# The last expert passes of a hybrid decoder step: the last gate ahead of the second square, one table change, and the scaling of two token tiles given to GpSimd and ScalarE

## The reference

```python
def rmsnorm(x, g):
    y = x * lax.rsqrt(jnp.mean(x * x, axis=-1, keepdims=True) + 1e-6)
    return y * g

# x: (536, 1024) after the mixer; u = rmsnorm(x, norm2_g)
h = (silu(einsum('btd,edf->btef', u, expert_w_gate))      # 16 experts, d = 1024, f = 256
     * einsum('btd,edf->btef', u, expert_w_up))
h = h * combine[..., None]                                # the top 1 of 4 groups, the top 2 in it
x = x + einsum('btef,efd->btd', h, expert_w_down)
y = rmsnorm(x, final_norm_g)
```

## Time and profile before

| | us |
|---|---|
| median of 3 runs | 812.83 (811.8 to 813.1) |
| the profiled execution | 816.96 |
| its span | 815.3 |
| PE busy (matmuls) | 782.8 (96%) |
| DVE busy | 431.7 (53%) |
| ACT busy | 208.4 (26%) |
| POOL busy | 38.8 (5%) |
| DMA moved | 126.89 MB, mean 156 GB/s |

### The profile page before, as it was taken

How to read it: one execution, slowest core, us unless ns; L and a number is a source line. 1 busy time by engine, 2 the same in 40 slices (tenths; PEclk the granted TensorE clock), 3 DMA queues, 4 the chain that set the end, 5 groups by cost and what they waited for, 6 DMA issues and landing times.

```text
span 815.3 us, 19720 instructions
## 1 busy us (share of the span) xinstructions
PE 782.8 (96%) x8426; PEld 539.0 (66%) x8426; DVE 431.7 (53%) x856; ACT 208.4 (26%) x488; POOL 38.8 (5%) x49
## 2 busy tenths in 40 slices
PE   7999999999999999999999999999999789999984
PEld 6877777787767877777777877767788533333321
DVE  5775667588768565657566455356114431111225
ACT  3122222254523312221212332220022401111134
POOL 0000000000000000000000000000000112222121
PEclk9999999999999999999999999999999889999997
DMA  9531432432212101201230102073935689999963
GB/s 341 202 113 51 137 107 71 176 105 65 91 52 80 53 28 55 68 15 61 81 104 28 51 32 80 2 266 162 384 116 207 220 326 400 390 403 393 349 224 136
DMA packets 36389, 126.89 MB, mean 156 GB/s; under 512 B 5736, under 2 KB 16008, under 8 KB 31440
## 3 DMA queue, kind: packets, MB, share of 16 engines
q1 hardware_dynamic: 32416, 115.78, 37.8%
q0 software_dynamic: 3888, 9.87, 4.3%
HBM read 106.31 MB, written 18.68 MB: 153 GB/s over the span
## 4 chain that ended last, share of the span: by engine, by line
PE 89%; DVE 4%; DMA 3%; issue 2%; ACT 1%; SPq 0%; POOL 0%; POOLq 0%; DVEq 0%; ACTq 0%
PE psum L1357 23%; PE psum L1338 12%; PE psum L1677 9%; PE psum L2554 9%; PE psum L2586 4%; PE psum L1315 4%; PE psum L1291 2%; PE psum L1302 2%; PE psum L1545 2%; PE psum L1633 1%; DVE arena L2019 1%; PE psum L1558 1%; PE psum L2534 1%; PE psum L1377 1%; PE psum L1442 1%
## 5 line engine op out<-in xcount | busy, mean ns | idle before, releaser
L2019 DVE TENSOR_TENSOR arena<-arena 128x512 f32<-128x512 f32 (+10 forms) x312 | 170.3, 546 | 50.8 <-ACT arena L1776 31.5
L1357 PE MATMUL psum<-arena 128*128 128x268 f32 x784 | 189.5, 393 | 0.0
L1357 PEld LDWEIGHTS psum<-arena 128*128 128x128 f32 x784 | 145.1, 189 | 37.8 <-issue 11.6
L1776 ACT ACTIVATE arena<-psum 128x268 f32<-128x268 f32 (+4 forms) x213 | 84.9, 406 | 282.6 <-PE psum L1357 146.6
L2019 DVE TENSOR_TENSOR arena<-psum,arena 128x256 f32<-128x256 f32 (+5 forms) x170 | 71.7, 425 | 80.9 <-PE psum L1558 21.8
L1338 PE MATMUL psum<-arena 128*128 128x268 f32 x392 | 105.0, 402 | 0.0
L1677 PE MATMUL psum<-arena 128*128 128x268 f32 x384 | 91.0, 391 | 1.6 <-DVE arena L2019 1.2
L2554 PE MATMUL psum<-arena 128*32 128x512 f32 (+1 forms) x640 | 86.2, 601 | 0.5 <-DVE arena L2707 0.3
L1338 PEld LDWEIGHTS psum<-arena 128*128 128x128 f32 x392 | 69.7, 189 | 20.4 <-issue 6.3
L1677 PEld LDWEIGHTS psum<-arena 128*128 128x128 f32 x384 | 71.1, 189 | 17.7 <-issue 3.3
L2707 DVE TENSOR_TENSOR arena<-psum,arena 128x256 f32<-128x256 f32 (+2 forms) x38 | 24.3, 663 | 104.4 <-ACT arena L2621 90.9
(11 more groups left out here) (205 smaller groups left out, 710.0 us busy)
## 6 DMA issues: line engine op xcount, KB each, us to landing
arena<-in_w_gu SPq DMA_DIRECT2D x16, 2048.0 KB, 21.6
arena<-in_w_in SPq DMA_DIRECT2D x46, 512.0 KB, 4.3
arena<-in_w_dn SPq DMA_DIRECT2D x16, 1024.0 KB, 20.6
arena<-in_w_out SPq DMA_DIRECT2D x2, 2048.0 KB, 14.6
arena<-arena SPq DMA_DIRECT2D x5, 536.0 KB, 5.2
arena<-in_x SPq DMA_DIRECT2D x8, 268.0 KB, 4.6
arena<-arena SPq DMA_DIRECT2D x16, 134.0 KB, 4.3
arena<-in_x SPq DMA_DIRECT2D x1, 2144.0 KB, 14.5
```

The source lines that it names most:

```text
L1357: last = mm(ps, w[:, k, :], x[:, k, :], start=(k == 0 and i in (0, 1, 3)), stop=(k == KD // 2 - 1), skip_group_check=i not in (0, 1, 3))
L1776: run(nc.scalar.activation(out, in_, fn, **kw), s)
L2019: run(v.tensor_tensor(out, a, b, op), s)
```

## The change

Four things change, all in the loop's last part.

1. ScalarE: `gate(11)` and `hidden_out(10)` come behind square(0) and ahead of the one Sqrt table load; root(0) comes after that, then squares and roots 1 and 2, then `hidden_out(11)`.
2. VectorE: `hidden(11)` comes ahead of all norms. `summed(0)`, with its wait for all late gathers, comes ahead of normed(2); summed(1) ahead of normed(4). For tiles 3 and 4 `normed` does only the reciprocal.
3. GpSimd: the three late gathers are issued only when tiles 0 and 1 have landed. When the gathers have landed, GpSimd multiplies tiles 3 and 4 by `g_row` into `ug`. ScalarE scales them by the reciprocal root with a Copy, in place, between its squares (`scaled(t)`), and SyncE writes these two to y from `ug`.
4. Two semaphores are new: `z_gx` (GpSimd to ScalarE) and `z_gy` (ScalarE to SyncE).

```diff
--- before.py
+++ after.py
@@ -49,6 +49,7 @@
 LATER = HT - EARLY * P
 LG0, PS0, ID0 = 0, 192, 320
 LATE = 3
+GAINED = 3
 SHIFT_TILES = 14
 RET0, GA0, GB0 = 14, 30, 38
 
@@ -939,6 +940,8 @@
         z_rt = sem("z_rt")
         z_rc = sem("z_rc")
         z_y = sem("z_y")
+        z_gx = sem("z_gx")
+        z_gy = sem("z_gy")
         z_out = [sem(f"z_out{i}") for i in range(2)]
 
         def rows_of(t):
@@ -2471,10 +2474,15 @@
                         n = rows_of(t)
                         sp.dma_start(xf[0:n, t, :], x2_dram[t * P:t * P + n, :]).then_inc(z_x[t], 16)
                     for t in range(TT):
-                        at_least(sp, z_y, TT + LATE, t + 1)
+                        n = rows_of(t)
+                        if t < GAINED:
+                            at_least(sp, z_y, GAINED + LATE, t + 1)
+                            y = xf[0:n, t, :]
+                        else:
+                            at_least(sp, z_gy, TT - GAINED, t - GAINED + 1)
+                            y = ug[0:n, t - GAINED, :]
                         sp.nop(nofuse=True)
-                        n = rows_of(t)
-                        sp.dma_start(O["y"][t * P:t * P + n, :], xf[0:n, t, :]).then_inc(z_out[t % 2], 16)
+                        sp.dma_start(O["y"][t * P:t * P + n, :], y).then_inc(z_out[t % 2], 16)
                     for j in range(LATE):
                         at_least(sp, z_late[j], 16, 16)
                     sp.nop(nofuse=True)
@@ -2504,19 +2512,25 @@
                                                 compute_op=ALU.add).then_inc(q_yd[e % 2], 16)
                     for q in range(2):
                         then(q_yd[q], ADDS[q], ADDS[q])
+                    then(z_x[0], 16, 16)
+                    then(z_x[1], 16, 16)
                     for j in range(LATE):
                         e = FIRST_LATE + j
                         pool.indirect_dma_start(late[:, j, :], None, x2_dram,
                                                 bass.IndirectOffsetOnAxis(ap=ids[:, e:e + 1], axis=0),
                                                 bounds_check=T - 1, oob_is_err=False).then_inc(z_in, 16)
                     then(z_in, 16 * LATE, 16 * LATE)
-                    for t in range(TT):
+                    then(z_x[2], 16, 16)
+                    then(q_tr, PIECES, parts_in(NPASS - 1))
+                    for t in range(GAINED, TT):
                         then(z_x[t], 16, 16)
+                        n = rows_of(t)
+                        nc.gpsimd.tensor_tensor(ug[0:n, t - GAINED, :], xf[0:n, t, :], g_row[0:n, :], ALU.mult).then_inc(z_gx, 1)
 
                     then(z_out[0], 48, 48)
                     then(z_out[1], 48, 48)
                     for j in range(LATE):
-                        then(z_y, TT + LATE, TT + j + 1)
+                        then(z_y, GAINED + LATE, GAINED + j + 1)
                         e = FIRST_LATE + j
                         pool.indirect_dma_start(O["y"], bass.IndirectOffsetOnAxis(ap=ids[:, e:e + 1], axis=0), fin[j], None,
                                                 bounds_check=T - 1, oob_is_err=False).then_inc(z_late[j], 16)
@@ -2662,30 +2676,29 @@
                         if i:
                             hidden_out(i - 1)
                             rows_out(i - 1)
-                    tables = [0]
-
-                    def table(fn):
-                        if tables[0]:
-                            at_least(act, z_sq, 3, tables[0])
-                        a(dummy, eps2[:, :], fn).then_inc(z_sq, 1)
-                        tables[0] += 1
-
                     gate(NPASS - 2)
                     hidden_out(NPASS - 3)
-                    table(ACT.Sqrt)
-                    for t in range(2):
+                    square(0)
+                    gate(NPASS - 1)
+                    hidden_out(NPASS - 2)
+                    a(dummy, eps2[:, :], ACT.Sqrt).then_inc(z_sq, 1)
+                    root(0)
+                    for t in range(1, 3):
                         square(t)
                         root(t)
-                    table(ACT.Sigmoid)
-                    gate(NPASS - 1)
-                    hidden_out(NPASS - 2)
-                    table(ACT.Sqrt)
-                    square(2)
-                    root(2)
                     hidden_out(NPASS - 1)
+                    def scaled(t):
+                        n = rows_of(t)
+                        at_least(act, z_gx, TT - GAINED, t - GAINED + 1)
+                        at_least(act, z_rc, TT + LATE, t + 1)
+                        y = ug[0:n, t - GAINED, :]
+                        a(y, y, ACT.Copy, scale=rs[0:n, t:t + 1]).then_inc(z_gy, 1)
+
                     for t in range(3, TT + 2):
                         square(t)
                         root(t)
+                        if GAINED < t <= TT:
+                            scaled(t - 1)
                     x = late[:, LATE - 1, :]
                     at_least(act, z_half, 1, 1)
                     at_least(act, z_ss, TT + LATE, squares[0])
@@ -2743,6 +2756,8 @@
                         n = x.shape[0]
                         at_least(dve, z_rt, TT + LATE, norms[0])
                         v.reciprocal(rs[0:n, t:t + 1], rs[0:n, t:t + 1]).then_inc(z_rc, 1)
+                        if GAINED <= t < TT:
+                            return
                         at_least(dve, z_rc, TT + LATE, norms[0])
                         v.scalar_tensor_tensor(y, x, rs[0:n, t:t + 1], g_row[0:n, :], ALU.mult, ALU.mult).then_inc(z_y, 1)
 
@@ -2765,15 +2780,15 @@
                                             AX.X, ALU.add).then_inc(q_ws, 1)
                         if 0 < i < NPASS - 2:
                             rows_in(i + 1)
+                    hidden(NPASS - 1)
                     normed(0)
                     normed(1)
-                    hidden(NPASS - 1)
-                    normed(2)
                     at_least(dve, z_in, 16 * LATE, 16 * LATE)
                     summed(0)
+                    normed(2)
                     normed(3)
+                    summed(1)
                     normed(4)
-                    summed(1)
                     normed(TT)
                     for q in range(2):
                         x = late[:, LATE - 1, 512 * q:512 * q + 512]
```

## The result

The changed kernel takes 818.08 us (median of 6 runs, 817.15 to 819.04), the kernel before 813.15 us beside it; the ratio is 1.0048, 95% interval 1.0032 to 1.0065. It is slower by 0.48%, where 0.25% less was forecast; 818.08 lies outside the range of 809.0 to 814.3. In the profiled executions the spans are 815.4 and 815.3 us, so two things have to be explained: what the change does in its trace, and why the kernel before is usually 3 to 4 us faster (medians of 812.8 to 813.8 us) than the execution of 816.96 us that the prediction was made on.

A forecast was written before the change was run, and what follows sets the result against it. It took TensorE's hole before down(10), then VectorE, then GpSimd's three scatters to bound the end. Down(11) gains 4.7 us, over half lost again; the third scatter starts 2.0 us sooner, 810.8 us for the median, range 809.0 to 814.3.

The forecast's parts named there:

- the first term of the sum: Last gate moved ahead on ScalarE: TensorE's idle 3.11 us before down(10) go, and the clock's fall (1.57 us) with them.
- L: Time when all late gathers are in, which summed(0) and GpSimd's products wait for: 794.3, 3.6 us after the last issue.
- the gathers are late: Rival: late gathers land later, delaying the end one to one; at 799.6 the time is 816.1 us; chance 0.12.
- Products and exclusion: GpSimd's two products take 2.6 us each and exclude VectorE products with two SBUF inputs; normed(2) held from 795.8 to 797.4.
- One table load: On ScalarE three loads of 1.28 us become one; its queue is through some 4 us sooner, which alone moves no end.
- The clock: TensorE's granted clock stays at 1.00 up to 799, without the fall to 0.50 behind the hole before down(10).

The follow-up runs named there:

- a_free_vector: The changed kernel with gathers issued as before and all five token tiles normed on VectorE: 813.75 us, ratio 1.0000 against the kernel before.
- a_store: The changed kernel with the first store of y held until the gathers have landed: 815.59 us, ratio 1.0016 against the kernel before.
- a_free: The changed kernel with its gathers issued as before, ahead of the landing of tiles 0 and 1: 814.28 us, ratio 1.0003 against the kernel before.
- c_early: The changed kernel, gathers issued as before, summed(0) waiting for the first alone, GpSimd products ahead of its wait for the gathers: 812.61 us, ratio 0.9982.
- b_wait: The kernel before with only the two GpSimd waits added (gathers issued once tiles 0 and 1 have landed): 816.63 us, ratio 1.0036.
- a_vector: The changed kernel with all five token tiles normed on VectorE, gathers still late: 817.34 us, ratio 1.0043 against the kernel before.
- a_norm_late: The changed kernel with normed(0) and normed(1) behind summed(0) on VectorE: 820.24 us, ratio 1.0079 against the kernel before.
- b_again3: The kernel before, unchanged, in a fourth profile: one execution of 814.10 us.
- b_again2: The kernel before, unchanged, in a third profile: one execution of 816.31 us.

## Why the prediction was wrong, point by point

- **The baseline.** The sum was made against one execution, of the late form, and I took the difference over to the median as if form and median had nothing to do with each other. That execution was 4.1 us over the median of the runs, and I noted it without asking what it was. In the early form the gate is in time by itself. So moving it, the first term of the sum, is right in its trace (gate at 786.7, no hole, down(10) 3.66 us), and no gain over the median was measured for it: a_free_vector, which has it together with the one table load and the new order, is at 1.0000 (0.9990 to 1.0010). That the median is of the early form is argued, as said above.
- **The step that failed: L.** "From issue to landing ... I take near the low end, 3.6" was 7.3 us. The issues themselves were right (787.05 is g+7.5, forecast g+7.25), and tile 1 alone did come early. Of the 3.7 us between them 0.8 is there in a_store too, where only the gathers move then (4.4 us). Another 0.8 is the third issue, which took 1.77 us beside VectorE's norm of tile 0 (789.38 to 790.66); I had read that very hindrance off the scatter in the earlier trace rows and applied it only to the products. The rest, up to 2.1 us, goes to the stores of y tiles 0 and 1, which the later gathers now meet. The earlier trace rows had them: of q1's 2.10 MB in 787 to 797 only 1.06 MB were tiles by my own count, so the other 1.04 MB were these two stores. I used them for the rate and left them out of what had still to move. With them, 3.18 MB at 0.32 MB/us from 787 on give 797.0 for the last gather in place of 793.7, an estimate that is 1.2 us under what came (g+16.2 against g+17.5). L came 3.9 us later than forecast, counted from g.
- **The rival "the gathers are late"** was the case that happened, with 0.12. Its rule, one to one in L, gives g+31.9 for the last scatter (27.95 + 3.9); 31.2 was measured. With the right L the sum is 0.7 us off, profile against profile, and one of its last steps was another than forecast: all three scatters followed the store of tile 4, and normed(6) held none of them up. From the first tile's load to the last scatter it is 29.4 us in the changed kernel (781.38 to 810.77) and 28.4 in the first profile of the kernel before, but 26.1 to 26.4 in the early form. That is 1.0 us against the one form and 3.0 to 3.3 against the other; 3.9 us were measured by the ratio, and the profiled execution of the changed kernel is itself 0.9 us under the median of its runs.
- **Products and exclusion** were right. A lone product takes 2.36 us; forecast 2.6. Half of the 4497 ns that the Trainium skill, "GPSIMD Engine Reference", section Performance versus the Vector engine, has for 2048 columns was the estimate of 2.25, which is nearer. Normed(2) starts at 798.44 and takes 2.47 us, 0.2 us less than what GpSimd's first product still needs (to 797.47 + 2.36 = 799.83) plus its own 1.29; the second product, of 24 rows, takes 3.34 us by the groups view, having waited for VectorE in its turn. This is the strong form of the rule in the Trainium skill's "SBUF — State Buffer", section SBUF: two separate sides: the trace agrees, and VectorE got in between the two products. The groups view of GpSimd in the changed kernel:

```profile
L2528 POOL TENSOR_TENSOR arena<-arena 24x1024 f32<-24x1024 f32 x1 | 3.3, 3342 | 0.0
L2528 POOL TENSOR_TENSOR arena<-arena 128x1024 f32<-128x1024 f32 x1 | 2.4, 2356 | 5.9 <-DMA arena<-x_rows,ids 5.9
```

  By a_free against a_free_vector (1.0003 and 1.0000) giving the two tiles away nets to nothing that can be measured.
- **One table load** came as forecast. No run has it alone; ScalarE's wait of 6.19 us behind it says that it moved no end in the changed kernel.
- **The clock** was forecast at 2.4 GHz throughout. It fell in the hole before down(11), which made that product 2.6 us longer (6.25 against 3.64), hidden behind VectorE's norm of late tile 5.

## What to carry to other kernels

A wait that is put before a transfer is priced by the landing of the last transfer behind it, beside all that moves at the new time; here the later gathers met the stores of the first normed tiles. Where a profiled execution is slower than the median by more than the change is worth, profile the kernel again before summing on its holes. When several transfers share one semaphore, look at who needs only the first: the one version here that is faster than the kernel before beyond its interval, by 0.2%, has it split.

## What the runs showed of the hardware

- A GpSimd two-tensor product and a VectorE product with both inputs in SBUF exclude each other for their whole length, to within 0.3 us (VectorE 1.29 becomes 2.02 to 3.19 us; GpSimd's 128x1024 product goes from 2.36 to 3.32 in c_early, where it starts 0.20 us into VectorE's norm of tile 1). Sums whose first input is in PSUM run beside a product at 1.26 to 1.29 us. GpSimd of c_early:

```profile
L2525 POOL TENSOR_TENSOR arena<-arena 128x1024 f32<-128x1024 f32 x1 | 3.3, 3320 | 5.0 <-DMA arena<-x_rows 5.0
```

- The issue of an indirect DMA is held too when it starts inside such a VectorE product: it then ends 0.85 to 0.90 us behind the product's end and takes 1.70 us (second gather of b_wait), 1.77 (third of the changed kernel) or 1.84 (third of a_vector). Issues that start 0.10 and 0.16 us before the product take 1.03 and 0.99, and the product keeps its 1.29 (a_store).
- The same five loads and three gathers land in two patterns from one execution to the next: tile 1 is there 5.6 to 6.0 us or 8.4 us behind the first load's issue. What decides was not found. Without gathers beside them the loads differ as well: the first gather, which waits for tile 1, starts 5.7 us behind the first load's issue in the changed kernel and 7.0 to 7.3 us behind it in a_vector, a_store, b_wait and a_norm_late.
- After pauses of TensorE of 1.0, 1.7 and 1.9 us the clock stayed at 2.4 GHz (b_wait, b_again3, a_store), and once after 3.11 us too: the window of b_wait behind that pause, with the clock third from the end,

```profile
799.70:803.30 3.60, 3.56 (x32) 1.13 (x32) 3.56 (x4) 1.38 (x3) 0.00 (x0) 1.00 0.40 154
```

  It fell in or just behind pauses of 3.11 us in the first profile, of 3.91 us in the changed kernel and of 4.42 us in a_vector, and behind one of only 2.54 us in b_again2, where down(10) took 5.35 us and the windows view shows 0.50 from 796 to 798:

```profile
794.21 0.44 PE L2563 MATMUL psum<-arena 128*128 128x128 f32 x2 [2.54 <-DVE arena L2707]
794.58 5.35 PE L2586 MATMUL psum<-arena 128*64 128x512 f32 x16
```

  So the length of the pause alone did not decide: 2.54 us lowered the clock in one execution, and 3.11 us left it in another.
